# x scaled in place and transposed plainly in the opening, squares shared out anew, and the second pair of up-weights loaded ahead of the gates, in a hybrid attention and DeltaNet layer

## The reference, cut to what matters

```python
# x: (1, 1024, 1024) float32
h = rms_norm(x, norm_w)                       # x * rsqrt(mean(x*x) + 1e-6) * norm_w
proj = jnp.einsum('bsd,de->bse', h, w_in)     # one combined projection, 6152 columns
qa, ka, va, za, qb, kb, vb, zb, ab, bb, gate = jnp.split(proj, split_points, axis=-1)
ya = diff_attention(qa, ka, va, ...) * silu(za)
ob = gated_deltanet(qb, kb, vb, ab, bb, ...)  # short conv, then chunked recurrence
yb = rms_norm(ob, gdn_norm_w) * silu(zb)
gates = sigmoid(gate)
merged = gates[:, :, 0] * (ya @ w_up_da) + gates[:, :, 1] * (yb @ w_up_gdn)
x = x + merged @ w_out
```

## Time and profile before

| | |
|---|---|
| time, median of 3 runs | 976.75 us (975.55 to 977.16) |
| profiled execution, its own time | 974.82 us |
| its span, first to last instruction | 973.1 us |
| mean granted TensorE clock | 0.998 |
| PE busy | 955.6 us (98%) |
| DVE, ACT, POOL busy | 538.6, 362.4, 273.5 us |
| DMA, mean over the span | 60 GB/s |

### The profile page before, as it was taken

The page is one execution under the profiler, slowest core; times in us unless marked ns, Lnnn a source line. Parts: engine busy times, 40 slices in busy tenths (PEclk is TensorE's granted clock), DMA queues, the critical chain, the costliest instruction groups (busy, mean ns, idle before and its releaser), DMA issues.

```text
span 973.1 us, 15462 instructions
## 1 busy us (share of the span) xinstructions
PE 955.6 (98%) x5451; PEld 791.1 (81%) x5451; DVE 538.6 (55%) x1322; ACT 362.4 (37%) x769; POOL 273.5 (28%) x213
## 2 busy tenths in 40 slices
PE   7999999999999999999999999999999999999998
PEld 6888888888788888887887888888888777887887
DVE  4667777647455646645626465565556574552112
ACT  5422232343333433432335455545545651112110
POOL 4233223353122222122134133132231222222221
PEclk9999999999999999999999999999999999999999
DMA  6012211212211211220111011111011113224332
GB/s 223 23 43 54 54 43 43 53 46 54 67 55 33 66 57 32 66 66 23 55 33 33 23 33 32 23 33 34 23 35 32 54 66 97 86 97 152 112 126 108
DMA packets 71191, 58.11 MB, mean 60 GB/s; under 512 B 3330, under 2 KB 61916, under 8 KB 71132
## 3 DMA queue, kind: packets, MB, share of 16 engines
q1 hardware_dynamic: 69840, 55.20, 19.6%
q10 hardware_dynamic: 1292, 2.14, 0.8%
HBM read 48.92 MB, written 8.40 MB: 59 GB/s over the span
## 4 chain that ended last, share of the span: by engine, by line
PE 89%; DVE 4%; issue 2%; ACT 2%; POOL 1%; DMA 1%; ACTq 0%; DVEq 0%; POOLq 0%
PE PS L1239 20%; PE PS L1237 20%; PE PS L1241 20%; PE PS L1561 3%; PE PS L1586 3%; PE PS L1676 3%; PE PS L1678 3%; PE PS L1677 3%; PE PS L1579 2%; PE PS L1214 1%; PE PS L1405 1%; PE PS L1398 1%; DVE gam L1867 1%; PE PS L1304 1%; PE PS L1424 1%
## 5 line engine op out<-in xcount | busy, mean ns | idle before, releaser
L621 POOL TENSOR_TENSOR w_lo<-w_raw,w_hi 128x512 fp32r<-128x512 f32 x130 | 189.4, 1457 | 581.2 <-ACT w_hi L772 581.2
L1239 PE MATMUL PS<-h_lo,w_hi 128*128 128x512 f32 x784 | 314.7, 401 | 0.0
L1237 PE MATMUL PS<-h_hi,w_hi 128*128 128x512 f32 x784 | 312.7, 399 | 1.9 <-DVE h_lo L1718 1.6
L1241 PE MATMUL PS<-h_hi,w_lo 128*128 128x512 f32 x784 | 313.7, 400 | 0.0
L1237 PEld LDWEIGHTS PS<-h_hi,w_hi 128*128 128x128 f32 x784 | 147.5, 188 | 31.6 <-issue 2.1
L1239 PEld LDWEIGHTS PS<-h_lo,w_hi 128*128 128x128 f32 x784 | 147.6, 188 | 27.6 <-issue 0.7
L1241 PEld LDWEIGHTS PS<-h_hi,w_lo 128*128 128x128 f32 x784 | 147.7, 188 | 27.2 <-issue 0.8
L772 ACT ACTIVATE w_hi<-w_raw 128x512 fp32r<-128x512 f32 x130 | 81.6, 629 | 178.5 <-PE PS L1241 109.5
L2043 DVE TENSOR_REDUCE mx<-PS 128x1 f32<-128x1024 f32 (+7 forms) x64 | 48.4, 756 | 49.6 <-PE PS L1566 49.6
L1777 DVE SCALAR_TENSOR_TENSOR acc<-pre,cw,acc 128x1024 f32<-128x1024 f32 x36 | 57.2, 1588 | 1.3
L1064 ACT ACTIVATE prob<-PS,nm,r_qk 128x1024 f32<-128x1024 f32 (+7 forms) x64 | 52.6, 829 | 5.5 <-DVE nm L2047 5.3
(11 more groups left out here) (253 smaller groups left out, 1358.1 us busy)
## 6 DMA issues: line engine op xcount, KB each, us to landing
w_raw<-in_w_in SPq DMA_DIRECT2D x98, 256.0 KB, 2.8
x_in<-in_x SPq DMA_DIRECT2D x8, 512.0 KB, 7.1
gate_a<-gate_dram SPq DMA_DIRECT2D x8, 512.0 KB, 4.2
w_raw<-in_w_out SPq DMA_DIRECT2D x16, 256.0 KB, 3.2
x_res<-in_x SPq DMA_DIRECT2D x8, 512.0 KB, 4.7
out<-out_sb SPq DMA_DIRECT2D x16, 256.0 KB, 2.2
gate_dram<-gate_st SPq DMA_DIRECT2D x7, 512.0 KB, 2.9
grow<-g_dram ACTq DMA_DIRECT2D x8, 256.0 KB, 3.3
```

Source lines behind the costliest of these rows:

```text
L621: pool.tensor_tensor(w_lo[:, b, :], w_raw[:, b, :], w_hi[:, b, :].bitcast(F32), ALU.subtract)\
L1237: pe.matmul(dst, w, hi, start=first, stop=False)
L1239: pe.matmul(dst, w, lo, start=False, stop=False)
L1241: mm = pe.matmul(dst, lo_w, hi, start=False, stop=last)
```

## The change

The diagonal matrices are gone. DVE multiplies each token tile of x by its factor where it lies (`scale_rows`), and PE transposes the blocks against the identity. ACT takes the squares of six tiles, DVE those of two. ACT issues one DMA for norm_w, which brings it directly as a column per channel block (128 partitions by 8 single elements, 512 bytes apart in memory); the eight loads of `vec_rows` go to SP's queue, behind x, and their transpose and copy to the end of the first projection tile. POOL's first weight splits wait until tile 3 of x is scaled. An ACT instruction on one column of the identity stands ahead of the squares. PE's warming matmuls are 14, not 10. PE's list for the first tile is a table: five groups, then groups and the transposes of the second half, by pairs of token tiles. The work on lambda moves behind the convolutions. In stage D the loop's first round is written out: both pairs of up-weights, then both gates.

```diff
-        WARM = 10
+        SQ_DVE, SQ_ACT = (0, 4), (1, 2, 3, 5, 6, 7)
+        WARM = 14
...
# SP
             for t in range(NT // 2, NT):
                 load_x(t)
+            for row, rows in VEC_ROWS:
+                load_vec(row, 0, rows)
+            for row, rows in ((58, da_q_gain), (59, da_k_gain)):
+                load_vec(row, SUB, rows)
...
-            with sp.Fori(0, NK // 2) as j:
+            for b in range(2):
+                load_up(b)
+            for b in range(2):
+                load_gate(0, b)
+            with sp.Fori(1, NK // 2) as j:
                 for b in range(2):
                     load_up(j * 2 + b)
                     load_gate(j, b)
...
# POOL
             for t in range(NT):
                 row_pow(t)
                 if t == NT // 2 - 1:
+                    pool.wait_ge(x_scaled.sem, x_scaled.at(NT // 2 - 1))
                     for b in range(2):
                         split_lo(0, b)
...
# ACT
-            for row, src in VEC_ROWS:
-                act.dma_start(vec_rows[row:row + src.shape[0], 0:src.shape[1]], src).then_inc(vec_loaded.sem, 16)
-            for row, src in ((58, da_q_gain), (59, da_k_gain)):
-                act.dma_start(vec_rows[row:row + 1, SUB:P], src).then_inc(vec_loaded.sem, 16)
+            act.dma_start(vec[:, 48:56], norm_w[0].rearrange("(k p) -> p k", p=P), allow_slow_non_contiguous=True).then_inc(norm_loaded.sem, 16)
+            act.wait_ge(consts_ready.sem, 2)
+            act.activation(act_junk[:, :], ident[:, 0:1], ACT.Square).then_inc(table_ready.sem, 1)
...
                 if n == 0:
-                    act.wait_ge(vec_ready.sem, 1)
+                    act.wait_ge(norm_loaded.sem, 16)
...
-            square_rows(1)
-            diagonal(0)
-            diagonal(1)
-            square_rows(3)
-            diagonal(2)
-            diagonal(3)
+            for t in range(1, NT // 2):
+                square_rows(t)
             for b in range(2):
                 split_hi(0, b)
+            for n in range(5):
+                round_h(n)
             square_rows(5)
-            for n in range(NK):
+            square_rows(6)
+            round_h(5)
+            square_rows(7)
+            for n in range(6, 2 * NK):
                 round_h(n)
-                if n == 1:
-                    square_rows(7)
-                    diagonal(4)
-                    diagonal(5)
...
# PE
+                return pe.transpose(PS[:, h_bank(n), (t % 4) * P:(t % 4 + 1) * P], x_in[:, t, k * P:(k + 1) * P], ident[:, :])
...
+            OPENING = [(5, 0, (0, 1)), (6, 0, (2, 3)), (7, 0, (4,)), (7, 1, (0, 1, 2, 3)), (8, 0, (5,)), (9, 0, (6,)),
+                       (10, 0, (7,)), (10, 1, (4, 5)), (12, 1, (6, 7))]
             first_tile = projection(0, 0, first=True)
+            first_half()
+            done = 0
+            for until, pair, ks in OPENING:
+                take(first_tile, 3 * (until - done))
+                done = until
+                for k in ks:
+                    second_half(k, pair)
+            take(first_tile, 46 - 3 * done)
+            pe.wait_ge(consts_ready.sem, N_CONSTS)
             pe.wait_ge(vec_loaded.sem, 16 * (len(VEC_ROWS) + 2))
+            pe.wait_ge(h_lo_ready.sem, h_lo_ready.at(2 * NK - 1))
             pe.transpose(PS[:, 7, 0:60], vec_rows[0:60, :], ident[0:60, 0:60]).then_inc(vec_T.sem, 1)
-            pe.wait_ge(consts_ready.sem, N_CONSTS)
-            first_half()
-            take(first_tile, 6)
-            for k in range(NK):
-                take(first_tile, 3)
-                second_half(k)
             whole(first_tile)
...
# DVE
+            def scale_rows(t):
+                dve.wait_ge(row_r_ready.sem, row_r_ready.at(t))
+                dve.tensor_scalar(x_in[:, t, :], x_in[:, t, :], row_r[:, t:t + 1], None, ALU.mult).then_inc(x_scaled.sem, 1)
```

92 lines of the change are left out of this document (48 added, 44 removed).

## The result

The changed kernel takes 965.8 us (median of four executions, 965.66 to 965.91). The kernel before, timed beside it, takes 976.95 (four executions, 975.55 to 977.96). The ratio is 0.9891, with a 95% interval of 0.9879 to 0.9904: 11.15 us faster, where 10.0 was forecast, and 965.8 us where 966.8 was. Later sets of executions put the kernel before at 976.0, 975.4 and 976.1, and the changed one once more at 965.8. The profiled executions are 974.82 and 965.91 us, 8.9 apart. So there are two things to explain: where 8.9 us went, and why the medians lie 2.2 us further apart. Part of the 2.2 is the draw of four executions: over all 50 executions of the kernel before that were timed the median is 975.9, which is 10.1 above the changed kernel and 1.2 more than the 8.9.

The account below looks back on a forecast made before the run. PE was taken as the bound, busy 955.6 of 973.1 us. The opening's 7.2 and stage D's 2.8 make 10.0, taken from the median 976.75: 966.75, stated as 966.8 us, with an 8-in-10 range of 964.4 to 970.5.

Parts of the forecast that it names:

- The transposes: Opening, PE: 64 plain transposes at 0.10 each cost 6.4 us less in all, 3.2 of it in the second half.
- The chain of the first half: Opening: x tiles scaled at 7.8, 9.4, 10.9, 12.45; first group at 14.9 behind w_lo, 3.9 us earlier.
- The second half: Opening: tiles scaled at 17.5, 19.7, 21.15, 22.7; second tile at 32.3, not 39.46, without w_lo wait; 7.2 us saved.
- The first convolution: After the first tile: DVE's later parameter copy delays it about 1.5 us against PE; DVE catches up within a tile or two.
- The load of norm_w: Opening DMA of 1024 single elements: at most 0.015 us each, landing taken as 10 us, no cost.
- (b): Opening: norm_w's load takes turns with x's rows; costs 2.0 us, 968.8 us; chance 0.17.
- (e): Opening: norm_w's single elements cost DMA time ahead of x, making the kernel slower; 979.6 us at 0.2 us each; chance 0.02.
- Stage D: Second output tile: earlier up-weight loads give w_lo at 798.3, PE's wait goes entirely; 2.8 us saved, 1.5 if y_lo slips.
- Rival (d): Stage D: POOL's earlier w_lo holds up y_lo and PE waits for that; 1.3 of 2.8 lost, 968.1 us; chance 0.11.
- Rival (c): Opening: PE's clock falls through gaps with only transposes between, slowing the first groups; costs 1.3, 968.1 us; chance 0.15.
- The sum: Whole kernel: 7.2 from the opening plus 2.8 from stage D, 10.0 us off the median 976.75, gives 966.75.
- 970.3 for two rivals together: Upper side of the 8-in-10 range: two of (b), (c) and (d) occurring together put the kernel at 970.3 us.

Follow-up runs that it names:

- e6_transposes_twice: The changed kernel with each of the 64 transposes of x issued twice in a row; 968.17 us.
- e2_dve_order: The changed kernel with DVE's work on lambda and the unit matrices moved to between the rests of h 11 and 12; 964.96 us.
- e3_norm_behind: The changed kernel with norm_w's element-wise load issued by SP behind the first weight slabs, not by ACT ahead of x; 965.75 us.
- e10_norm_twice: The changed kernel with norm_w's element-wise load issued twice on ACT's queue, once into columns that nothing reads; 966.34 us.
- e4_opening_only: The changed kernel with stage D's loads put back behind the first gates, the opening still changed; 971.5 us.
- e5_before_warm14: The kernel before with 14 warming matmuls in place of 10 and nothing else; 975.78 us, ratio 0.9998.
- e11_params_chain: The kernel before with norm_w loaded directly, the other parameters behind the first tile, lambda's exponential and differences behind split and convolutions; 975.45 us, ratio 0.9996.
- e8_pow_between: e2_dve_order with POOL's power of token tile 4 put between its first two w_lo, not behind both; 965.12 us.

## Why the prediction was right

**The transposes.** Right at 0.10 each. The prediction had 3.2 us of them on PE's path in the second half. e6_transposes_twice shows 2.1 in its profile and 2.4 in its time for all of them.

**The chain of the first half.** Forecast scaled at 7.8, 9.4, 10.9, 12.45; measured 7.5, 10.0, 11.5, 13.0 (each L1727 start and 0.75). The pace of 1.5 is right. The second is 0.6 late, since x's second tile lands 1.1 late behind the load of norm_w, which the prediction had costed at nothing. The first group starts at 15.36 and not at 14.9, for the reason given: it waits for w_lo. That this chain replaces one that began with the parameters' landing is borne out by the 9.9 us between the two in three profiles. How its 3.45 us divide between the parameters, the scaling in place, the new shares of the squares and the warm-up is not shown.

**The second half.** Forecast 17.5, 19.7, 21.15, 22.7 and the second tile at 32.3; measured 17.85, 19.99, 21.47, 22.94 and 32.87. The 7.2 of the sum are 6.6. The wait for w_lo at the second tile goes, as forecast.

**The first convolution.** Here a step failed. "DVE is busy 55% of the span and catches up within a tile or two" was to make the late convolution free. It is 2.3 us later against PE, not 1.5, since lambda's sums and the reductions stand behind the parameters too; and before DVE catches up, ACT's tanh has delayed one slab's split and PE has waited. That costs 0.6 of the 6.6, and e2_dve_order gets it back. A mean busy share says nothing of the one moment at which the queue stands.

**The load of norm_w.** "No cost" holds, but its working does not. It landed at 5.9 us and not at 10, at 0.009 us for each element, inside the bound of 0.015. It delays x by 1.1, and the net price is nothing because what stands behind (tile 4 of x, the squares beside POOL) takes the gain back when the load is put elsewhere (e3_norm_behind). Rivals (b) and (e) fell: x was never held up by whole rows, and ACT's first rounding did not wait for norm_w.

**Stage D.** Forecast w_lo at 798.3 on the old time; measured 792.65, which is 798.7 with the 6.0 of the opening added. y_lo did slip beside it, from 2.49 to 3.58 for four, and still ended in time (at 793.19; PE's last matmul with a y_lo of that tile starts at 793.82), so the wait went entirely: 2.9 against 2.8 in the profiles. Rival (d) saw the slip and not that there was room for it. The term was under-sized all the same. Taken out or put back alone, the edit is worth 4.4 and 5.7 between medians. For the 5.7 the profile gives the reason, a wait that is 1.2 longer and a clock that falls behind it. For the 4.4 it doesn't: there stage D gave 2.9.

**The clock.** Rival (c) fell: the clock was at 1.00 from 4.6 to 20 in the changed kernel; ahead of 4.6 the warming matmuls start 0.21 apart. The Trainium skill says that transposes of this mode don't count as activity for the clock (TensorE: Matmul & The Clock Gate, PE-mode transpose). By that rule the clock would have been down when the groups began; the windows from 5 to 15 us, with transposes alone from 7.6 on, don't show that. In e3_norm_behind and e10_norm_twice it did fall, 1.3 and 0.2 us into the groups, and there PE had also stood idle for 2.3 us behind the transposes, against 1.2 in the changed kernel. Which of the two brings it is not told apart here.

**The sum.** In the profiles 6.6 - 0.6 + 2.9 = 8.9, against 10.0 forecast. In the medians it is 11.15. The prediction made its sum on one execution of the kernel before and subtracted it from the median, which leaves whatever the median has over that execution untouched. So 965.8 against 966.8 is the work of two errors of opposite sign, 1.1 too much for the profile's part and 2.2 left out, and that they nearly cancel is luck. Of the 2.2, 1.0 is the draw of the first four executions of the kernel before. For the other 1.2 there are three candidates, each seen in a profile: the clock that falls in stage D (1.5 us in e4_opening_only and e5_before_warm14), parameters that land early or late (0.8 us), and a clock that comes up late in the opening (e11_params_chain). In what share of the executions each occurs is not shown. The prediction's 970.3 for two rivals together is 970.1 by its own terms, which changes nothing.

The fastest kernels of this study are e2_dve_order and e8_pow_between, at 964.96 and 965.12 us.

## What to carry to other kernels

Where a wait on the bounding engine is to be removed, look at several executions of it: the clock that it is granted behind the wait, and how late the transfer lands, can double what the wait costs, and one profile may show neither. When work is moved from the head of a stage to its end, write down what each engine has queued behind it there: with lambda's exponential left ahead of a weight split, the move of the parameters cost 6 us, 2.1 of them as a wait and 2.8 through a clock that was low behind it. Where a run is to show that a chain was no bound, look at the pace of the engine behind it first: in e11_params_chain another bound had taken its place, and the time stood still. An engine freed earlier meets another one at work: with DVE and POOL both on operands in memory, starting one sooner paid nothing three times.
